# Sliding attention of one block: sink column, shared normalising, reordered first and last steps

## The reference, cut to what matters

```python
q, k, v, z = split(u @ w_in)                 # 1024, 256, 256, 1024 columns
q = rope(rmsnorm(q, q_gain), pos)            # per head of 64
k = rope(rmsnorm(k, k_gain), pos)
s = q @ k.T * 64 ** -0.5                     # 4 query heads share one k head
s = where(band of 128 keys, s, -inf)
m = maximum(s.max(-1), sink)                 # one learned sink per head
e = exp(s - m)
p = e / (e.sum(-1) + exp(sink - m))
y = ((p @ v) * silu(z)) @ w_out
```

## Time and profile before

| | us |
|---|---|
| runs: median, lowest, highest (3 runs) | 3581.74, 3576.57, 3582.09 |
| profiled execution | 3581.5 |
| its span | 3579.7 |
| mean granted PE clock, share of full speed | 0.981 |
| attention stretch of the first window | from 2111.4 to 2189.8 |

### The profile page before, as it was taken

How to read it: one execution, slowest core, us unless ns; L and a number is a source line. 1 busy time by engine, 2 the same in 40 slices (tenths; PEclk the granted TensorE clock), 3 DMA queues, 4 the chain that set the end, 5 groups by cost and what they waited for, 6 DMA issues and landing times.

```text
span 3579.7 us, 43838 instructions
## 1 busy us (share of the span) xinstructions
PE 3428.3 (96%) x16635; PEld 2707.3 (76%) x16635; DVE 1999.8 (56%) x4682; ACT 714.6 (20%) x1766; POOL 87.9 (2%) x106
## 2 busy tenths in 40 slices
PE   8987999999999999999999988999999999999988
PEld 3484788888845568888888866888887888887766
DVE  4472367554405784675545668643464657558566
ACT  2231021100014551211001144022112011131143
POOL 0000000000000000000000010000000000000110
PEclk9998999999999999999999999999999999999999
DMA  3200312222210003122222311212121222102311
GB/s 131 83 13 24 129 48 83 83 94 83 107 70 24 25 25 130 48 83 83 95 83 83 99 56 36 83 71 79 60 71 52 95 83 83 36 25 92 105 42 48
DMA packets 39976, 254.09 MB, mean 71 GB/s; under 512 B 5797, under 2 KB 5925, under 8 KB 11617
## 3 DMA queue, kind: packets, MB, share of 16 engines
q1 hardware_dynamic: 31616, 224.41, 17.6%
q0 software_dynamic: 3664, 15.07, 1.2%
q10 hardware_dynamic: 4496, 11.89, 1.2%
HBM read 242.68 MB, written 2.18 MB: 68 GB/s over the span
## 4 chain that ended last, share of the span: by engine, by line
PE 88%; DVE 8%; issue 2%; ACT 1%; DMA 1%; ACTq 0%; POOL 0%; POOLq 0%; DVEq 0%
PE PL L1224 26%; PE PX L1224 20%; PE PL L932 14%; PE PL L1570 4%; PE PL L1417 3%; PE PL L916 2%; PE PX L1679 2%; DVE SCR L3046 2%; PE PL L1335 1%; DVE SCR L3061 1%; PE PL L1595 1%; PE PX L1355 1%; PE PL L1722 1%; PE PX L942 1%; PE PL L897 1%
## 5 line engine op out<-in xcount | busy, mean ns | idle before, releaser
L932 PE MATMUL PL<-xn,ring 128*128 128x264 f32 (+1 forms) x1600 | 498.4, 469 | 10.9 <-DVE xn L2407 10.4
L932 PEld LDWEIGHTS PL<-xn,ring 128*128 128x128 f32 x1600 | 303.0, 191 | 191.7 <-issue 159.8
L2468 DVE TENSOR_TENSOR Z<-PL,SCR 128x512 f32<-128x512 f32 (+3 forms) x104 | 63.9, 614 | 430.3 <-PE PL L932 330.8
L1224 PE MATMUL PL<-Z,ring 128*128 128x256 f32 (+1 forms) x1200 | 286.4, 389 | 10.4 <-DVE Z L3438 8.6
L1224 PEld LDWEIGHTS PL<-Z,ring 128*128 128x128 f32 x1200 | 232.4, 194 | 48.3 <-DVE Z L3438 9.7
L1224 PE MATMUL PL<-AUX,ring 128*128 128x256 f32 (+1 forms) x1104 | 255.6, 380 | 0.0
L1224 PEld LDWEIGHTS PL<-AUX,ring 128*128 128x128 f32 x1104 | 209.7, 190 | 29.2 <-DVE AUX L2804 0.2
L1224 PE MATMUL PL<-xn,ring 128*128 128x264 f32 (+1 forms) x864 | 199.9, 383 | 1.2 <-DVE xn L2710 1.2
L1224 PEld LDWEIGHTS PL<-xn,ring 128*128 128x128 f32 x864 | 163.9, 190 | 28.1 <-DVE xn L2710 1.5
L1867 ACT ACTIVATE SCR<-PL 128x256 f32<-128x256 f32 (+1 forms) x72 | 27.7, 384 | 734.0 <-PE PL L1224 734.0
L1224 PE MATMUL PX<-Z,AUX 128*128 128x264 f32 (+1 forms) x704 | 163.8, 384 | 2.7 <-DVE Z L3246 2.7
(11 more groups left out here) (531 smaller groups left out, 6025.8 us busy)
## 6 DMA issues: line engine op xcount, KB each, us to landing
ring<-w_tiles SPq DMA_DIRECT2D x212, 1024.0 KB, 4.8
Z<-Z ACTq DMA_DIRECT2D x16, 264.0 KB, 5.1
SCR<-head_rows POOLq DMA_DIRECT2D x16, 264.0 KB, 3.7
AUX<-norm_scratch POOLq DMA_DIRECT2D x8, 528.0 KB, 6.5
cst<-consts ACTq DMA_DIRECT2D x1, 2188.5 KB, 15.2
resid<-x ACTq DMA_DIRECT2D x4, 512.0 KB, 8.9
Z<-norm_scratch POOLq DMA_DIRECT2D x4, 512.0 KB, 7.5
AUX<-mem POOLq DMA_DIRECT2D x2, 1024.0 KB, 5.2
```

Source lines behind the costliest of these rows:

```text
L932: mm = pe.matmul(PL[:, 2 * h + c, 0:e - a], ring[t % 2][:, k, P * h:P * h + P], src_block(name, k)[:, a:e], start=k == 0, stop=k == KB - 1)
L1224: mm = pe.matmul(ps, lhs(k), rhs(k), start=kc == 0 and k == 0, stop=kc == per - 1 and k == 3)
L2468: ins = dve.tensor_tensor(d, ps, f, ALU.mult)
```

## The change

- Row sums: blocks are taken in pairs, one to partitions 0-63 of `PX` and one to 64-127 (`sum_row64` slices become 64 wide; `qk_rows` and `pick64` have 74 rows). `w_rs` is then stored by four ACT copies.
- Gate unit 2 stands ahead of the key products on PE.
- The sink becomes one more column of `wS` (257 instead of 256), written by GpSimd; the exponential's row sum then holds it, and the two small DVE additions and the small exponential are gone. `wS` has four buffers.
- `normalise` on DVE covers heads 0 and 1; GpSimd does heads 2 and 3. `turn` goes head by head and waits for each half.
- scores(0), scores(1) stand ahead of gate units 6 and 7 on PE; DVE and ACT do bias_max(0), (1), exps(0), (1) and normalise(0) there.
- DVE's loop runs bias_max(m+2) ahead of normalise(m); `outputs` moves from ACT to DVE, two groups behind; the gate products follow two groups behind.
- Some semaphores are merged or renamed (`x_in` and `swap_in` become `act_in`).

```diff
 # PE: row sums
                 for b in range(10):
                     pe.wait_ge(wq_sq, 10 * i + b + 1)
+                    if b % 2 == 0:
+                        continue
                     for c, a, e in halves(T2):
-                        mm = pe.matmul(PX[0:20, c, 0:e - a], K("sum_row64", 18 - 2 * b, 38 - 2 * b), qk_sq[b][:, a:e],
-                                       start=b == 0, stop=b == 9)
+                        for x in range(2):
+                            mm = pe.matmul(PX[64 * x:64 * x + 64, c, 0:e - a], K("sum_row64", 9 - b, 73 - b),
+                                           qk_sq[b - 1 + x][:, a:e], start=b == 1, stop=b == 9)
...
 # PE: gate unit 2, key products
                 mm.then_inc(wq_tps, 1)
+                gate_part(2, 0, KB)
                 pe.wait_ge(pick_in, 16 * (i + 1))
...
-                gate_part(2, 0, KB)
-                for u in range(3, 8):
+                for u in range(3, 6):
                     gate_part(u, 0, KB)
...
 # PE: turn
-                    pe.wait_ge(wa_nrm, N_W * i + m + 1)
                     if m:
                         pe.wait_ge(wa_pt, N_W * i + m)
-                    for c, a in enumerate(range(k0, k1, P)):
-                        kn = min(P, k1 - a)
-                        for h in range(4):
+                    for h in range(4):
+                        if h % 2 == 0:
+                            pe.wait_ge(*((wa_upper, N_W * i + m + 1) if h else (wa_nrm, inverted(i, m) + 1)))
+                        for c, a in enumerate(range(k0, k1, P)):
...
                 scores(0)
                 scores(1)
+                gate_part(6, 0, KB)
+                gate_part(7, 0, KB)
                 pe.wait_ge(psum_free, evacuated(n + "_z"))
                 for m in range(N_W + 1):
                     if m + 2 < N_W:
...
 # ACT
-                for u in range(3, 8):
+                for u in range(3, 6):
                     open_gate(u)
...
                 exps(0)
+                exps(1)
+                open_gate(6)
+                open_gate(7)
                 for m in range(N_W):
-                    if m + 1 < N_W:
+                    if 2 <= m + 1 < N_W:
                         exps(m + 1)
                     turned(m)
-                    if m:
-                        outputs(m - 1)
-                outputs(N_W - 1)
...
 # DVE
                 def normalise(m):
...
                     dve.wait_ge(wa_exp, N_W * i + m + 1)
-                    step(dve.tensor_tensor(w_sm[j][0:nq], w_sm[j][0:nq], w_es[j][0:nq], ALU.add))
-                    step(dve.reciprocal(w_rc[j][0:nq], w_sm[j][0:nq]))
-                    for h in range(4):
+                    dve.reciprocal(w_rc[j][0:nq], w_sm[j][0:nq]).then_inc(wa_nrm, 1)
+                    dve.wait_ge(wa_nrm, inverted(i, m))
+                    for h in range(2):
...
+                def outputs(m):
...
+                    dve.wait_ge(wa_o, N_W * i + m + 1)
+                    src = PL[:, 2 + m % 2, 0:2 * nq].rearrange("p (x t) -> p x t", x=2)
+                    dve.tensor_copy(Z2[:, 12 + 2 * g:14 + 2 * g, P * q_tile:P * q_tile + nq], src).then_inc(wa_oc, 1)
+
                 bias_max(0)
-                for m in range(N_W):
-                    if m + 1 < N_W:
-                        bias_max(m + 1)
-                    normalise(m)
+                bias_max(1)
+                copy_out(n + "_z", 6)
+                normalise(0)
+                copy_out(n + "_z", 7)
+                for m in range(N_W + 2):
+                    if m + 2 < N_W:
+                        bias_max(m + 2)
+                    if 1 <= m < N_W:
+                        normalise(m)
+                    if m >= 2:
+                        outputs(m - 2)
                     if m in (4, 5):
                         weight_sums(n + "_out", 0, m - 4)
...
 # GpSimd
+                def sink(m):
...
+                    if m >= N_WS:
+                        pool.wait_ge(wa_tps, N_W * i + m - N_WS + 1)
+                    pool.tensor_copy(wS[m % N_WS][0:nq, :, k1 - k0], nsink[0:nq, s:s + 4]).then_inc(wa_sink, 1)
+
+                def normalise_upper(m):
...
+                    pool.wait_ge(wa_nrm, inverted(i, m))
+                    for h in range(2, 4):
+                        S = wS[j][0:nq, h, 0:k1 - k0]
+                        ins = pool.tensor_scalar(S, S, w_rc[j][0:nq, h:h + 1], K("ones", 0, 1)[0:nq], ALU.mult, ALU.mult)
+                    ins.then_inc(wa_upper, 1)
...
+                for m in range(N_WS - 1):
+                    sink(m)
+                for m in range(N_W):
+                    if m == 2:
+                        pool.wait_ge(wq_z, 8 * i + 8)
+                    normalise_upper(m)
+                    if m >= 2:
+                        gated(m - 2)
+                    if m + N_WS - 1 < N_W:
+                        sink(m + N_WS - 1)
+                gated(N_W - 2)
+                gated(N_W - 1)
```

More of the change, by code:

```diff
@@ L211, in build @@
         meta_sq = tiny[:, 0:8 * META].rearrange("p (b t) -> p b t", b=8)
-        x_in = [sem(f"x_in{j}") for j in range(4)]
+        act_in = [sem(f"act_in{j}") for j in range(4)]
         first_in, par_in, dn_rows = sem("first_in"), sem("par_in"), sem("dn_rows")
@@ L275, in build @@
             sem(n) for n in ("wq_cos", "wq_rope", "wq_tps", "wq_rs", "wq_kbc", "wq_kn", "wq_kd", "wq_z"))
-        swap_in, key_half = [sem(f"swap_in{j}") for j in range(3)], [sem(f"key_half{x}") for x in range(2)]
+        key_half = [sem(f"key_half{x}") for x in range(2)]
         na_rows, na_s, na_max, na_exp, na_nrm, na_tps, na_pt, na_v, na_done = (
@@ L509, in build, with inverted @@
         N_W = 4 * NT2
-        wS = [SCR[:, 1024 * j:1024 * (j + 1)].rearrange("p (h k) -> p h k", h=4) for j in range(3)]
-        wPT = [SCR[:, 3072 + 1024 * j:3072 + 1024 * (j + 1)].rearrange("p (c n) -> p c n", c=2) for j in range(2)]
-        w_nm, w_sm, w_es, w_rc = ([tiny[:, 16 * j + 4 * x:16 * j + 4 * x + 4] for j in range(3)] for x in range(4))
+        N_WS = 4
+        wS = [SCR[:, 1040 * j:1040 * (j + 1)].rearrange("p (h k) -> p h k", h=4) for j in range(N_WS)]
+        wPT = [SCR[:, 4160 + 1024 * j:4160 + 1024 * (j + 1)].rearrange("p (c n) -> p c n", c=2) for j in range(2)]
+        w_nm, w_sm, w_rc = ([tiny[:, 16 * j + 4 * x:16 * j + 4 * x + 4] for j in range(N_WS)] for x in range(3))
         w_rs = tiny[:, 112:212].rearrange("p (i r) -> p i r", i=5)
+        def inverted(i, m):
+            return 2 * (N_W * i + m) + 2
         def w_span(i):
@@ L794, in _ @@
             load(0, 0)
-            sp.wait_ge(x_in[3], 16)
+            sp.wait_ge(act_in[3], 16)
             load(1, 1)
@@ L2133, in window @@
                 act.wait_ge(wq_sum, i + 1)
-                act.activation(pair(qk_rows, T2), psb(PX[0:20], w_pair("sum", 0), T2), ACT.Sqrt, scale=1.0 / 64,
-                               bias=K("eps", 0, 1)[0:20]).then_inc(wq_root, 1)
+                act.activation(pair(qk_rows, T2), psb(PX[0:74], w_pair("sum", 0), T2), ACT.Sqrt, scale=1.0 / 64,
+                               bias=K("eps", 0, 1)[0:74]).then_inc(wq_root, 1)
                 for j, (rows, turned_rows) in enumerate(SWAPS):
@@ L2157, in window @@
                 at = w_pair("rs", 0)
-                act.activation(w_rs[:, 0:4, :], PX[:, at, 0:80].rearrange("p (i r) -> p i r", i=4), ACT.Copy, scale=-0.125)
-                act.activation(w_rs[0:META, 4, :], PX[0:META, at, 80:100], ACT.Copy, scale=-0.125).then_inc(wq_rs, 1)
+                for x in range(2):
+                    for nq, t0, t1 in ((P, 0, 4), (META, 4, 5)):
+                        rows = PX[0:nq, at, 74 * t0:74 * t1].rearrange("p (i r) -> p i r", r=74)[:, :, 64 * x:64 * x + 8]
+                        ins = act.activation(w_rs[0:nq, t0:t1, 0:16].rearrange("p i (g x e) -> p i g x e", g=4, x=2)[:, :, :, x, :],
+                                             rows.rearrange("p i (g e) -> p i g e", g=4), ACT.Copy, scale=-0.125)
+                ins.then_inc(wq_rs, 1)
                 open_gate(1)
@@ L2172, in exps @@
                     nq, k0, k1 = w_span(m // 4)
-                    j = m % 3
+                    j = m % N_WS
+                    act.wait_ge(wa_sink, N_W * i + m + 1)
                     act.wait_ge(wa_max, N_W * i + m + 1)
-                    act.activation(w_es[j][0:nq], w_es[j][0:nq], ACT.Exp)
                     for h in range(4):
-                        S = wS[j][0:nq, h, 0:k1 - k0]
+                        S = wS[j][0:nq, h, 0:k1 - k0 + 1]
                         ins = act.activation(S, S, ACT.Exp, scale=-1.0, bias=w_nm[j][0:nq, h:h + 1],
@@ L3590, in _constants @@
     c["sum_row"] = np.broadcast_to(np.arange(15)[None, :] == 7, (P, 15))
-    c["sum_row64"] = np.arange(38)[None, :] == 18 + p[:, None] // 64
+    c["sum_row64"] = np.arange(72)[None, :] == 8 + p[:, None] // 64
     c["eps"] = np.broadcast_to(np.array([EPS, 1.0, EPS * EPS])[None, :], (P, 3))
```

(2 more changed lines are left out.)

65 lines of the change are left out of this document (31 added, 34 removed).

## The result

The changed kernel takes 3616.81 us (median of 4 runs, 3610.97 to 3623.05) against 3581.57 before (4 runs): the ratio is 1.0103, 95% interval 1.0090 to 1.0117. It is slower by 35 us, in the direction and inside the range of the prediction, 15 us above its point.

A forecast was written before the change was run, and what follows sets the result against it. DVE's work set the 4.04 us group, PE having 0.69 slack; the new order makes a serial chain. Per window 14.5 - 4.35 + 0.3 = +10.4, two windows +20.9 on 3581.5: 3602 us, 8 in 10 range 3583 to 3630.

The forecast's parts named there:

- The loop: Steady attention groups: scores, bias_max, reciprocal, normalising and turn become one serial chain, period 5.4 us (5.05 to 5.8) against 4.04.
- GpSimd's part of it: Normalising in steady groups: GpSimd operations take 0.45 us each and hold DVE's second operation by about 0.27.
- The rival with GpSimd as slow as its product: Steady groups: GpSimd at 0.73 gives period 5.8, +6 us per window, 3614; chance 0.16, shared with serial row sums.
- The three parts of the stretch: Attention stretch from gates' end to output projection, cut into front, middle and back: together +14.5 us per window.
- front: Gates' end to the end of turn(3): 16.0 us before, 16.1 after, net +0.1.
- middle: Turns 3 to 13: 41.9 us before, ten periods of 5.4 make 54.0 after, net +12.1.
- back: End of turn(13) to the output projection: 20.0 us before, 22.3 after, net +2.3.
- the two weight-sum steps: DVE's weight sums in the attention stretch: hidden in DVE's idle time of some 1.9 us a group, at no cost.
- Row sums: Row-sum step of each window: paired matmuls overlap, -4.35 us, bounds 0 and -4.6; all that follows moves with the last sum.
- gate unit 2: Ahead of the key products: PE's stall of about 3.5 us now waits for DVE's copy-out; +0.3 us, bounds -1 and +1.
- the clock: Attention stretch: rival that PE's granted clock falls in the longer loop, period 7.0 at half clock, 3626 us; chance 0.14.
- The other side: Attention stretch: rival that DVE's relief pays in full, PE's 3.35 us becoming the period, -15.5 per window, 3551 us; chance 0.08.

The follow-up runs named there:

- the one-ahead order: Changed kernel with DVE's bias_max put back to one group ahead of normalise, all else as changed: 3543.05 us, ratio to before 0.9908.
- the gaps filled: Changed kernel with three extra 128x256 matmuls, product unused, on PE ahead of turn in groups 2 to 13: 3599.11 us, ratio to before 1.0067.
- run 40: Not a follow-up run: "run" is a verb here, for row-sum matmul pairs whose 40 records take 4.60 us where 9.01 was taken before.

## Why the prediction came out as it did

**The loop** was right. Period 5.4 forecast, 5.31 measured at the full clock in groups without weight sums; the chain runs through scores, bias_max, reciprocal, normalising and turn as forecast, DVE's idle time before bias_max shows it, and the one-ahead order removes it.

**GpSimd's part of it** was right in size by two errors. The forecast had DVE held by 0.27 and GpSimd at 0.45 each, a little behind. DVE was not held (0.62 for two; the forecast had 0.61 for two undisturbed), GpSimd took 1.35 for its two, and the chain runs through GpSimd: 1.36 + 0.04 + half a turn 0.66 = 2.06, where the forecast's leg was 0.61 + 0.27 + 0.06 + 1.03 = 1.97. The rival with GpSimd as slow as its product (0.73 each) came nearly true in its condition (0.68 each) and not in its price of 5.8, since DVE's operations and the first half of the turn ran meanwhile. The Trainium skill (SBUF — State Buffer, "Who interferes with whom") has a GpSimd operation and a DVE operation in a two-port mode exclude one another for the whole instruction. In which mode DVE's operations ran, no run here shows. The records agree that the engines lengthen one another's work, but one GpSimd operation, recorded as 0.82, lay wholly beside DVE's three, which took 1.03 in place of 0.87: a hold for a whole operation is not what they show.

**The three parts of the stretch**, first window: front +1.7 (forecast +0.1), middle +17.5 (2121.06 to 2180.41 is 59.35; forecast +12.1), back +2.5 (forecast +2.3), and 0.4 that lies between the three as cut here (turns 3 and 13 are both longer). The front's miss is mostly a group partly at half clock, 5.90 where the forecast had 4.6. With the gaps filled and nearly all of it at full clock, the middle is 54.2 (forecast 54.0) and the windows cost +15.3 and +16.3 (forecast +14.5). That the middle agrees to 0.2 is partly luck: the prediction hid the two weight-sum steps in DVE's idle time at no cost, and through GpSimd they cost 1.5, as much as before the change (5.31 and 4.30 for 4.04); the other eight groups, seven at 5.31 and one at 4.88 for 5.4, gave 1.2 of it back.

**Row sums and gate unit 2.** The sums were right: -4.41 a window (forecast -4.35). Of the gate unit the stall was right, with DVE's copy-out named as forecast, and the size was not: between the sums' end and the gates' end, moved scores left out, both windows take 64.3 us where they took 65.3, so -1.0 and not +0.3. In the first window -4.4, -1.0 and the stretch's +22.0 make the 16.65.

**The term that was mis-sized is the clock.** The prediction put it at nothing and gave its fall a chance of 0.14, on one row in which PE was busy 2.83 of 5 us at 1.00. In the changed kernel PE is busy 67 of 99 us with a wait of 1.7 us in each group, and the granted clock goes to 0.50 for one to three groups at a time, which then take 6.70 us. At 13 to 16 us by the filled gaps, this is about the 15 us by which the point was low: the kernel with the gaps filled lies at +21.7 us beside its runs of before, and the prediction's sum was +20.9. That the rest agrees so closely is in part the smaller errors above, which cancel. The rival was priced at 12 us a window (half of the time at half clock); against the filled gaps the windows lost 6.8 and 9.7.

**The other side.** The rival in which DVE's relief pays, at 3551 us, came true in the one-ahead kernel: 3543. The relief was there; the order threw it away.

## What to carry to other kernels

Before running a consumer further ahead, write down what each of its instructions waits for and what stands behind that wait: a deeper lookahead on one engine alone, with its producer's order unchanged, turned two overlapping engines into one serial loop. (Whether PE's scores a group further ahead as well would open it again was not run.) Where a change lengthens a wait of PE, price the granted clock as well, and try the same order with the gaps filled to tell the two apart. An engine that is relieved gains only where its inputs are already there: look at what it will wait for next. And work put into the idle time of one engine on the loop may still lengthen the loop through another: DVE's weight sums held up GpSimd.

## What was not expected of the hardware

- The granted clock fell to 0.50, for one to three groups at a time, in a loop in which PE was busy about two thirds of the time, with a wait of 1.7 us in each group and none above 2.2 in the stretch; with 1.6 us of extra matmuls in the same gaps it was 1.00 from 2120 to 2174.
- Two GpSimd operations with one tensor and two scalars on 128x256 take 1.35 us, on average nearly as long as the two-tensor product's 0.73; one alone takes 0.82 and three take 1.78, beside three and one of DVE's. Beside DVE's two-tensor additions on 128x512 the two take up to 2.38.
- Matmul pairs to 64 output partitions each run 40 records in 4.60 us where 40 records to 20 partitions took 9.01, half the time for the same number of records.
